# Second-half masked copies, ScalarE's copy of the queries' rope part, and GpSimd's subtraction of four levels' exponents, in the first mixer of a two-block model kernel

## The chip, the cores and the metric

The kernel is one program on one core of a Trainium2 chip. The metric is device time in microseconds (us) of one execution; lower is better. Five engines run their own instruction streams and meet at semaphores: TensorE (PE; its weight loads are listed apart as PEld), VectorE (DVE), ScalarE (ACT), GpSimd (POOL) and SyncE (SP, which issues DMAs). SBUF is the on-chip memory, PSUM the eight banks that TensorE writes to.

## The reference, cut to what matters

Two models of two layers follow each other, d_model 1024, batch 1, all float32. The sequence is 256 frames, with 16 meta tokens put in front in the first model: T = 272 columns. The change lies in one place, the first layer's mixer, which has two halves that read the same projection `z = rmsnorm(h) @ w_in`.

The first half is a gated linear recurrence (`hgrn2_mixer`), 4 heads of 128 keys and 128 values, in chunks of 64 tokens (the 16 meta tokens are a chunk of their own):

```python
b = jnp.cumsum(gi, axis=2)                        # sums of log decays in the chunk
diff = b[:, :, :, None, :] - b[:, :, None, :, :]
dec = jnp.exp(jnp.where(tri, diff, -jnp.inf))
att = jnp.einsum('bhtk,bhtsk,bhsk->bhts', qi, dec, ki)
o_intra = jnp.einsum('bhts,bhsv->bhtv', att, vi)
```

The second half is attention with low-rank queries and keys (`mla_mixer`), 4 heads; a head's query has 128 plain columns and 64 that are rotated (the rope part), and is normed over all 192 with a gain `qn_g` before the rotation.

Both halves' outputs go through `w_out`. What follows (the layer's MLP, the second layer and the second model) is not touched.

## The kernel before, in words

**Data.** Activations are kept feature by token: a tile holds 128 features by 272 tokens, and [128, 4, 272] holds all four heads. Weights come from HBM in units of up to 128x1024 through four buffers RAW (SP, `load_unit`). ScalarE copies a unit to a rounded half WH (`act_split`, L346) and VectorE subtracts it to get the rest, WL (`dve_split`, L353); each product is three matmuls (UH by WH, UL by WH, UH by WL; `products`, L368, and `products_rows`, L380). There are seven WH and WL buffers. Unit n of RAW is loaded once WL of unit n-4 is made; WH of unit n once the matmuls of unit n-7 are done. In the first mixer the units are: 10 and 11 the keys' and values' latent (`ckv`), 12 the keys' rope part (`kr`), 13 and 14 the queries (`qup`: plain and rope part), 15 the keys (`kvup` 0), 16 to 19 the recurrence's values (`hi`), 20 to 23 its gate (`hg`).

**The levels.** `att` inside a chunk can't be one product, since `dec` depends on both tokens. It is built in seven levels. Level 0 is the diagonal. Level number j (1 to 6) has the half size h = 1, 2, 4, 8, 16, 32: tokens are cut in blocks of 2h, and level j gives the pairs with the key's token s in a block's first half and the query's token t in its second half. With B the running sums and r the last token of the first half, the factor is exp(B[r]-B[s]) for a key and exp(B[t]-B[r]) for a query, both at most 1. For i = 0 to 5 (h = 1 to 32):

- `exponents(i)` on VectorE (L1145 to 1155) writes those two differences into E (even i) or HG (odd i); it waits for `scan` (B) and, from i = 2, for `op` i-2, which has read that buffer. For h up to 8 it is 2 instructions of 128x544, for h = 16 and 32 it is 8 of 128x128 (four heads, two halves).
- `exponents(i)` on ScalarE (L953 to 956) takes Exp of them in place.
- `operands(i)` on VectorE (L1157 to 1170) multiplies K and Q by them into KB and QB; it waits for ScalarE's Exp and until TensorE has read the last level's KB and QB (`mix atm`).
- `level(i)` on TensorE (L688, and L694 for the meta tokens) multiplies KB by QB: 16 weight loads and 16 matmuls of 128x128 into two PSUM banks.
- `attention(i+1)` on VectorE (L1177 to 1193) copies from these banks into ATT [128 keys' tokens, 8, 128 queries' tokens] where the mask `lev` of the level is set (`copy_predicated`, 2 instructions of 128x512, L1187), and likewise for the meta tokens (L1192). The masks of levels 1 to 6 have no bit in first halves of t.

**The queries' rope part.** TensorE's `up("qup", 1, ...)` leaves it in four PSUM banks. ScalarE's `query_rest` (L985) squares it into TMA (mark `hsq q 1`). VectorE's `query_rest` (L1253 to 1256) waits for that and copies it times the gain into QR (mark `gr q`). The banks are free for the keys' product `kvup` 0 at `gr q`; `kvup` 0 also needs the banks of the plain part, which ScalarE copies at L977.

**Order.** The order on each engine is written out by hand; there is no planner. VectorE, from the scan on: exponents 0, WL 11, exponents 1, operands 0, the latent's low parts (CL, L1197), attention 0, exponents 2, WL 12, CL, operands 1, attention 1, exponents 3, CL, `latent_pairs` (L1225), WL 13, `key_rest` (L1261), operands 2, attention 2, `latent_means` (L1207), exponents 4, WL 14, operands 3, attention 3, `latent_roots` (L1213 to 1218), exponents 5, WL 15, `query_rest`, operands 4, attention 4, the chunk's decay (L1396 to 1399), WL 16 and 17, `keys` (L1268), operands 5, attention 5, `head_pairs` q (L1231), attention 6, `head_pairs` k, WL 18, KD (L1413), and so on. TensorE: intra 0, `ckv` 1, level 0, `kr`, level 1, `latent_sums` (L709), `qup` 0, level 2, `qup` 1, level 3, `spread_columns` l (L746), `kvup` 0, level 4, values (0,0) (L380), level 5, values (0,1) with the queries' sums between (L724), `keys_turned` (L679, needs KD), further values, `rotate`. ScalarE around the change: Exp 0, WH 12, Exp 1, CH 2 (L970, L971), Exp 2, CH 3, WH 13 and 14, Exp 3, square of KR (L1048), WH 15, a root (L1051), the plain queries' copy and square (L977, L980), Exp 4, WH 16 and 17, `query_rest`, Exp 5, RKV (L1060), WH 18, the keys' square (L1064). GpSimd has only memsets: seven at the start of the mixer (L624 to 628) and two for the second model (L1698, L1699). SP only loads.

Of the kernel before, what the change touches and what calls it, by code (L numbers as in the profile page):

```python
# [8 lines left out]
T = 272  # L9
# [269 lines left out]
def program(nc, xin, pin, gains, cst, wpack, out):  # L279
# [13 lines left out]
    with ctx:  # L293
# [28 lines left out]
        def g(name, j=0, p=128):  # L322
            return G[0:p, GAT[name] + j:GAT[name] + j + 1]
# [297 lines left out]
        def gpsimd_mixer(p):  # L621
            for i, (z, val) in enumerate(((QB[:, :, :], 0.0), (KB[:, :, :], 0.0), (ATT[:, :, :], 0.0), (ATM[:, :, :], 0.0),
                                          (E[:, :, :], 1.0))):
                p.e.memset(z, val).then_inc(*p.mark("zero", i))  # L624
            p.wait_ge("zero", 4)
            p.e.memset(E[:, :, 0:1], 0.0).then_inc(*p.mark("zero", 5))
            p.wait_ge("zero", 5)
            p.e.memset(E[:, :, 16:T:64], 0.0).then_inc(*p.mark("zero", 6))


        def tensor_mixer(t):
# [144 lines left out]
            def rotate(key, src, nh):  # L776
                t.wait_ge("gr", key)
                b = banks.take(t, ("rot", key), ("rsin", key), nh)
                for hh in range(nh):
                    ins = t.e.matmul(PS[0:64, b + hh, 0:T], c("rot", p=64), src[:, hh, :], start=True, stop=True)  # L780
                ins.then_inc(*t.mark("mix", "rot", key))
# [88 lines left out]
            level(2)  # L870
            up("qup", 1, [(0, 0), (1, 1)], 64, ("gr", "q"))
            level(3)
# [78 lines left out]
        def scalar_mixer(a):  # L951
            def exponents(i):
                h, ee = LEVELS[i], EB[i % 2]  # L953
                rng = slice(0, T) if h <= 8 else slice(16, T)
                a.wait_ge("ex", i)
                a.e.activation(ee[:, :, rng], ee[:, :, rng], ACT.Exp).then_inc(*a.mark("exp", i))
# [25 lines left out]
            def query_rest():  # L982
                b1 = banks.at["qup", 1]
                a.wait_ge("mix", "qup", 1)
                a.e.activation(QRSQ[:, :, :], PS[0:64, b1:b1 + 4, 0:T], ACT.Square).then_inc(*a.mark("hsq", "q", 1))  # L985

# [153 lines left out]
        def vector_mixer(v):  # L1140
# [5 lines left out]
            def exponents(i):  # L1146
                h, ee = LEVELS[i], EB[i % 2]
                v.wait_ge("scan")
                if i > 1:
                    v.wait_ge("op", i - 2)  # L1150
                for (bl, br, ref), (el, er, _) in zip(halves(B, h), halves(ee, h)):
# [25 lines left out]
            def attention(level):  # L1177
# [5 lines left out]
                if level:  # L1183
                    v.wait_ge("att", level - 1)
                for x in range(2):
                    src = PS[:, b + x, :].rearrange("p (n t) -> p n t", t=128)
                    ins = v.e.copy_predicated(ATT[:, 4 * x:4 * x + 4, :], m, src)  # L1187
                if level <= 4:
# [63 lines left out]

            def query_rest():  # L1253
                b = banks.at["qup", 1]
                v.wait_ge("hsq", "q", 1)
                v.e.tensor_scalar(QR[:, :, :], PS[0:64, b:b + 4, 0:T], g("qr", 0, 64), None, ALU.mult).then_inc(
                    *v.mark("gr", "q"))

            def key_rest():
# [25 lines left out]
            def rotated(key, rr, nh):  # L1285
# [3 lines left out]
                v.wait_ge("c")  # L1289
                v.wait_ge("gr", key)  # L1290
                v.wait_ge("mix", "rot", key)
# [79 lines left out]
            attention(0)  # L1371
            exponents(2)
            dve_split(v, 13)
            latent(1, 0)
            operands(1)
            attention(1)
            exponents(3)
            latent(1, 1)
# [5 lines left out]
            latent_means()  # L1384
            exponents(4)
            dve_split(v, 15)
            operands(3)
            attention(3)
            latent_roots()
            exponents(5)  # L1390
            dve_split(v, 16)
            query_rest()
            operands(4)
# [1571 lines left out]
```

## Time and profile before

| | us |
|---|---|
| median of 3 runs | 1263.34 (1263.01 to 1263.54) |
| profiled execution: span of the instructions | 1261.9 |
| the profiled execution's own time beside its span | not listed; the median of the runs is 1.44 over the span |
| busy in the span: PE, PEld, DVE, ACT, POOL | 1231.6, 1206.4, 908.1, 737.1, 6.4 |
| granted TensorE clock, mean | 0.994 of full speed |
| DMA | 205.51 MB, mean 163 GB/s |

Busy times are sums over instructions that overlap a little in their pipelines, so the step from one instruction's start to the next one's start is the better price where an engine runs without a pause. "Idle before" is the pause in front of an instruction with what released it. PEld, the weight loads, shows TensorE's pauses more plainly than the matmuls, whose ends are modelled.

### The profile page before, as it was taken

What the parts mean: (1) busy time and instruction counts of PE and PEld (TensorE: products, weight loads), DVE (VectorE), ACT (ScalarE), POOL (GpSimd) and SP (SyncE); (2) the same over time, 40 slices, a digit from 0 to 9 for tenths busy, and PEclk for the clock granted to TensorE, in tenths of its full rate; (3) what the DMA queues carried; (4) which work ended last, traced back from release to release, by engine and by line L of the source; (5) the groups of instructions that cost most, each with busy time, mean ns of one, the idle gap of its engine ahead of it and who ended that gap; (6) DMA issues with size and microseconds to landing.
All of it is one profiled execution on the core that took longest, in us unless ns stands there. A gap on an engine that the chain in (4) does not pass through costs nothing.

```text
span 1261.9 us, 24318 instructions
## 1 busy us (share of the span) xinstructions
PE 1231.6 (98%) x10110; PEld 1206.4 (96%) x10110; DVE 908.1 (72%) x1571; ACT 737.1 (58%) x1257; POOL 6.4 (1%) x16
## 2 busy tenths in 40 slices
PE   8999999999999999999999999999999999999997
PEld 8889799999999999999999999999888899999997
DVE  6896566665446776444876899966788768999656
ACT  6753456664445765334555666655766866665655
POOL 1000000000000000000000000000000000000000
PEclk9999999999999999999999999999899999999999
DMA  7223244555552655553663666574364236665640
GB/s 275 72 101 105 64 164 148 192 181 180 174 168 98 216 186 185 184 184 126 218 195 119 193 194 199 159 238 134 120 225 159 89 117 192 193 189 188 215 141 34
DMA packets 59753, 205.51 MB, mean 163 GB/s; under 512 B 6739, under 2 KB 9340, under 8 KB 59516
## 3 DMA queue, kind: packets, MB, share of 16 engines
q1 hardware_dynamic: 57536, 201.21, 49.0%
q10 hardware_dynamic: 2108, 2.75, 0.7%
q8 instruction: 80, 1.31, 0.4%
q14 instruction: 29, 0.24, 0.1%
HBM read 202.87 MB, written 1.06 MB: 162 GB/s over the span
## 4 chain that ended last, share of the span: by engine, by line
PE 85%; DVE 8%; ACT 4%; issue 1%; DMA 1%; DVEq 0%; ACTq 0%
PE PS L368 69%; PE PS L413 6%; DVE WL L353 2%; PE PS L380 2%; DMA RAW<-wpack 1%; ACT WH L346 1%; PE PS L462 1%; PE PS L2450 1%; ACT EE L2608 1%; PE PS L520 1%; PE PS L2517 0%; PE PS L688 0%; DVE X L1905 0%; ACT L532 0%; PE PS L402 0%
## 5 line engine op out<-in xcount | busy, mean ns | idle before, releaser
L353 DVE TENSOR_TENSOR WL<-RAW,WH 128x1024 fp32r<-128x1024 f32 (+2 forms) x387 | 460.6, 1195 | 211.3 <-ACT WH L346 210.8
L346 ACT ACTIVATE WH<-RAW 128x1024 fp32r<-128x1024 f32 (+2 forms) x387 | 392.3, 1033 | 218.6 <-PE PS L368 184.8
L368 PE MATMUL PS<-UH,WH 128*128 128x256 f32 (+1 forms) x1464 | 415.7, 284 | 7.6 <-DVE WL L353 3.8
L368 PE MATMUL PS<-UL,WH 128*128 128x256 f32 (+1 forms) x1464 | 414.9, 283 | 0.0
L368 PE MATMUL PS<-UH,WL 128*128 128x256 f32 (+1 forms) x1464 | 414.7, 283 | 0.0
L368 PEld LDWEIGHTS PS<-UH,WH 128*128 128x128 f32 x1464 | 276.6, 189 | 8.6 <-issue 3.4
L368 PEld LDWEIGHTS PS<-UH,WL 128*128 128x128 f32 x1464 | 276.9, 189 | 0.0
L368 PEld LDWEIGHTS PS<-UL,WH 128*128 128x128 f32 x1464 | 275.2, 188 | 0.0
L368 PE MATMUL PS<-HL,WH 128*128 128x272 f32 (+1 forms) x512 | 145.8, 285 | 0.0
L368 PE MATMUL PS<-HH,WH 128*128 128x272 f32 (+1 forms) x512 | 145.6, 284 | 0.0
L368 PE MATMUL PS<-HH,WL 128*128 128x272 f32 (+1 forms) x512 | 145.4, 284 | 0.0
L368 PE MATMUL PS<-FH,WH 128*128 128x256 f32 x352 | 98.5, 280 | 0.0
L368 PE MATMUL PS<-FL,WH 128*128 128x256 f32 x352 | 98.5, 280 | 0.0
L368 PE MATMUL PS<-FH,WL 128*128 128x256 f32 x352 | 98.5, 280 | 0.0
L368 PEld LDWEIGHTS PS<-HH,WL 128*128 128x128 f32 x512 | 96.6, 189 | 0.0
L368 PEld LDWEIGHTS PS<-HL,WH 128*128 128x128 f32 x512 | 96.3, 188 | 0.0
L368 PEld LDWEIGHTS PS<-HH,WH 128*128 128x128 f32 x512 | 96.1, 188 | 0.0
L413 PE MATMUL PS<-UH,WH 128*128 128x256 f32 (+1 forms) x240 | 68.7, 286 | 1.5 <-DVE UL L540 1.2
L413 PE MATMUL PS<-UL,WH 128*128 128x256 f32 (+1 forms) x240 | 67.6, 282 | 0.0
L413 PE MATMUL PS<-UH,WL 128*128 128x256 f32 (+1 forms) x240 | 67.6, 282 | 0.0
L368 PEld LDWEIGHTS PS<-FH,WH 128*128 128x128 f32 x352 | 66.2, 188 | 0.0
L368 PEld LDWEIGHTS PS<-FL,WH 128*128 128x128 f32 x352 | 66.2, 188 | 0.0
(409 smaller groups left out, 2066.1 us busy)
## 6 DMA issues: line engine op xcount, KB each, us to landing
RAW<-wpack SPq DMA_DIRECT2D x361, 512.0 KB, 4.2
RAW<-wpack SPq DMA_DIRECT2D x18, 384.0 KB, 3.5
RAW<-wpack SPq DMA_DIRECT2D x6, 256.0 KB, 2.7
C<-cst SPq DMA_DIRECT2D x1, 1072.0 KB, 5.9
HB<-bias_rows ACTq DMA_DIRECT2D x1, 1024.0 KB, 5.3
out<-X SPq DMA_DIRECT2D x4, 256.0 KB, 2.3
X<-xin ACTq DMA_DIRECT2D x2, 272.0 KB, 6.0
X<-xin SPq DMA_DIRECT2D x2, 272.0 KB, 5.9
```

Source lines behind the costliest of these rows:

```text
L346: a.e.activation(WH[n % NH][:, 0:w], RAW[n % NR][:, 0:w], ACT.Copy).then_inc(*a.mark("wh", n))
L353: v.e.tensor_tensor(WL[n % NH][:, 0:w], RAW[n % NR][:, 0:w], WH[n % NH][:, 0:w].bitcast(f32), ALU.subtract).then_inc(*v.mark("wl", n))
L368: ins = t.e.matmul(o, part(n, hw, kw, a, b), x(kx), start=first and not i and not p, stop=last and i == len(kcs) - 1 and p == 2)
L380: ins = t.e.matmul(o, x(kx), part(n, hw, kw, 0, w), start=not i and not p, stop=i == len(kcs) - 1 and p == 2)
L413: ins = t.e.matmul(PS[:, b, 0:w], part(n, hw, k, 0, 128), x_(k), start=k == 0 and p == 0, stop=k == 7 and p == 2)
L462: return t.e.matmul(o, src[:, m, a:z], ONE[:, 0:1], start=start, stop=stop)
L520: ins = t.e.matmul(PS[:, b, a:z], rooted(st, x).to_broadcast([128, 128]), ID[:, 0:z - a], start=True, stop=True)
L2450: ins = t.e.matmul(PS[:, b, 0:256], x[:, k, 128 * i:128 * i + 128], part(n, hw, kw, 0, 256), start=k == 0 and p == 0, stop=k == 7 and p == 2)
L2608: ins = a.e.activation(e, e, ACT.Exp, bias=s[:, 2 * i + m:2 * i + m + 1], scale=-1.0, accum_out=s[:, 4 + 2 * i + m:5 + 2 * i + m])
```

## The change

Four edits, all in the first mixer.

1. `exponents(i)` for i = 2 to 5 (h = 4, 8, 16, 32) leaves VectorE and is issued by GpSimd with the same tiles and shapes, in this order, each behind `op` i-2. Its mark is `exg`, and ScalarE's Exp of these four waits for it. 20 instructions in all: 2, 2, 8 and 8.
2. `attention` for levels 1 to 6 copies second halves of t only: one instruction over both banks, of 128 x 8 x (64/h) x h = 128x512 elements, in place of two of 128x512. Level 0 stays as it was, the meta tokens' copies too.
3. QR, the queries' rope part times its gain, is copied by ScalarE in its `query_rest`, ahead of the square, and VectorE's `query_rest` is gone. The banks of `qup` 1 are free at ScalarE's square.
4. The waits on QR go by ScalarE's new mark (`qn` 1).

```diff
@@ gpsimd_mixer
             p.e.memset(E[:, :, 16:T:64], 0.0).then_inc(*p.mark("zero", 6))
+            p.wait_ge("scan")
+            for i in range(2, 6):
+                h, ee = LEVELS[i], EB[i % 2]
+                p.wait_ge("op", i - 2)
+                for (bl, br, ref), (el, er, _) in zip(halves(B, h), halves(ee, h)):
+                    rb = ref.to_broadcast(list(bl.shape))
+                    p.e.tensor_tensor(el, rb, bl, ALU.subtract)
+                    ins = p.e.tensor_tensor(er, br, rb, ALU.subtract)
+                ins.then_inc(*p.mark("exg", i))
@@ tensor_mixer (and the same in VectorE's rotated)
-                t.wait_ge("gr", key)
+                t.wait_ge(*(("qn", 1) if key == "q" else ("gr", key)))
@@
-            up("qup", 1, [(0, 0), (1, 1)], 64, ("gr", "q"))
+            up("qup", 1, [(0, 0), (1, 1)], 64, ("hsq", "q", 1))
@@ scalar_mixer
-                a.wait_ge("ex", i)
+                a.wait_ge("ex" if i < 2 else "exg", i)
@@
                 a.wait_ge("mix", "qup", 1)
+                a.e.activation(QR[:, :, :], PS[0:64, b1:b1 + 4, 0:T], ACT.Copy, scale=g("qr", 0, 64)).then_inc(*a.mark("qn", 1))
                 a.e.activation(QRSQ[:, :, :], PS[0:64, b1:b1 + 4, 0:T], ACT.Square).then_inc(*a.mark("hsq", "q", 1))
@@ vector_mixer, attention
-                for x in range(2):
-                    src = PS[:, b + x, :].rearrange("p (n t) -> p n t", t=128)
-                    ins = v.e.copy_predicated(ATT[:, 4 * x:4 * x + 4, :], m, src)
+                h = 1 << level >> 1
+                if level == 0:
+                    for x in range(2):
+                        src = PS[:, b + x, :].rearrange("p (n t) -> p n t", t=128)
+                        ins = v.e.copy_predicated(ATT[:, 4 * x:4 * x + 4, :], m, src)
+                else:
+
+                    def second(z):
+                        return z.rearrange("p (n k s) -> p n k s", n=8, s=2 * h)[:, :, :, h:2 * h]
+                    mh = c("lev", 128 * level, 128 * level + 128).bitcast(u32).rearrange("p (k s) -> p k s", s=2 * h)[:, :, h:2 * h]
+                    k, w = mh.shape[1], mh.shape[2]
+                    ins = v.e.copy_predicated(second(ATT[:, :, :].rearrange("p n t -> p (n t)")),
+                                              mh.unsqueeze(1).to_broadcast([128, 8, k, w]),
+                                              second(PS[:, b:b + 2, :].rearrange("p x t -> p (x t)")))
@@ the order on VectorE
-            exponents(2)
...
-            exponents(3)
...
-            exponents(4)
...
-            exponents(5)
             dve_split(v, 16)
-            query_rest()
             operands(4)
```

## Rows read from the trace of the kernel before

**Rows 1.** The page: span, busy time by engine, chain that ended last.
```profile
span 1261.9 us, 24318 instructions
PE 1231.6 (98%) x10110; PEld 1206.4 (96%) x10110; DVE 908.1 (72%) x1571; ACT 737.1 (58%) x1257; POOL 6.4 (1%) x16
PE 85%; DVE 8%; ACT 4%; issue 1%; DMA 1%; DVEq 0%; ACTq 0%
```
**Rows 2.** Windows: length, busy PE, PEld, DVE, ACT, POOL, clock, DMA share, GB/s.
```profile
46.00:85.42 39.42, 33.73 (x298) 31.70 (x298) 38.61 (x89) 24.68 (x35) 0.00 (x0) 1.00 0.26 90
85.42:146.30 60.88, 60.88 (x471) 54.96 (x472) 39.85 (x61) 26.05 (x42) 0.00 (x0) 1.00 0.31 98
```
**Rows 3.** Timeline of TensorE's weight loads: start, length, [idle before <-releaser].
```profile
56.59 0.13 PEld L368 LDWEIGHTS PS<-UH,WH 128*64 128x64 f32 x1 [1.65 <-DVE CL L1197]
73.73 0.74 PEld L746 LDWEIGHTS PS<-ID,CO 128*128 128x128 f32 x6
75.88 0.19 PEld L368 LDWEIGHTS PS<-CH,WH 128*128 128x128 f32 x1 [1.41 <-DVE QR L1256]
78.93 1.86 PEld L688 LDWEIGHTS PS<-QB,KB 128*128 128x128 f32 x16
81.47 0.09 PEld L380 LDWEIGHTS PS<-WH,UH 128*16 128x16 f32 x1 [0.68 <-DVE WL L353]
85.42 1.86 PEld L688 LDWEIGHTS PS<-QB,KB 128*128 128x128 f32 x16 [1.34 <-DVE QB L1169]
```
**Rows 4.** VectorE's groups by form, 47 to 94 us: busy, mean ns.
```profile
L1187 DVE COPY_PREDICATED ATT<-C,PS 128x512 f32<-128x512 uint32 x14 | 9.4, 721 | 0.0
```
**Rows 5.** VectorE's timeline around steps of the sum (start, length).
```profile
47.06 0.73 DVE L1153 TENSOR_TENSOR E<-B 128x544 f32<-128x544 f32 x1
54.18 0.71 DVE L1153 TENSOR_TENSOR E<-B 128x544 f32<-128x544 f32 x1
55.45 0.67 DVE L353 TENSOR_TENSOR WL<-RAW,WH 128x512 fp32r<-128x512 f32 x1
68.61 0.72 DVE L1168 TENSOR_TENSOR KB<-K,HG 128x544 f32<-128x544 f32 x1 [0.71 <-PE PS L694]
71.74 0.28 DVE L1153 TENSOR_TENSOR HG<-B 128x128 f32<-128x128 f32 x1
73.36 1.22 DVE L353 TENSOR_TENSOR WL<-RAW,WH 128x1024 fp32r<-128x1024 f32 x1
74.49 1.34 DVE L1256 TENSOR_SCALAR QR<-PS,G 64x1088 f32<-64x1088 f32 x1
75.75 0.27 DVE L1168 TENSOR_TENSOR KB<-K,E 128x128 f32<-128x128 f32 x1
77.37 1.34 DVE L1187 COPY_PREDICATED ATT<-C,PS 128x512 f32<-128x512 uint32 x2
80.21 2.34 DVE L353 TENSOR_TENSOR WL<-RAW,WH 128x1024 fp32r<-128x1024 f32 x2
82.48 1.27 DVE L1268 TENSOR_TENSOR KN<-PS,ACC 128x1088 f32<-128x1088 f32 x1
91.57 1.27 DVE L1413 TENSOR_TENSOR K<-K,E 128x1088 f32<-128x1088 f32 x1
```
**Rows 6.** ScalarE's timeline: the plain queries' copy, and the rope part's square.
```profile
66.46 1.08 ACT L977 ACTIVATE QN<-PS 128x1088 f32<-128x1088 f32 x1 [0.43 <-PE PS L368]
73.00 1.05 ACT L985 ACTIVATE TMA<-PS 64x1088 f32<-64x1088 f32 x1
```
**Rows 7.** GpSimd's timeline: memsets at the start and late.
```profile
0.98 1.00 POOL L624 MEMSET QB<- 128x1088 f32 x1
1.92 1.00 POOL L624 MEMSET KB<- 128x1088 f32 x1
284.71 0.95 POOL L1698 MEMSET V0H<- 128x1024 f32 x1 [279.53 <-PE PS L368]
```
**Rows 8.** VectorE's timeline beside the last of these memsets.
```profile
285.05 1.49 DVE L1650 TENSOR_TENSOR HL<-TB,HH 128x272 fp32r<-128x272 f32 x4
```

More of the change, by code:

```diff
@@ L1148, in exponents @@
                 v.wait_ge("scan")
-                if i > 1:
-                    v.wait_ge("op", i - 2)
                 for (bl, br, ref), (el, er, _) in zip(halves(B, h), halves(ee, h)):
@@ L1251, in key_roots @@
                 v.e.reciprocal(KSC[:, :, :], KSC[:, :, :]).then_inc(*v.mark("hrec", "k"))
[L1253 to L1257, printed above, removed]
             def key_rest():
@@ L1289, in rotated @@
                 v.wait_ge("c")
-                v.wait_ge("gr", key)
+                v.wait_ge(*(("qn", 1) if key == "q" else ("gr", key)))
                 v.wait_ge("mix", "rot", key)
```

## The prediction

> **What bounds the kernel now.** I read the page first: TensorE is busy 98% of the 1261.9 us span, and the chain that ended last runs 85% on TensorE, 8% on VectorE [rows 1]. So VectorE's work is free except where TensorE pauses for it, and the question is whether the first mixer is such a place. The windows say so, and where it stops: from 46.00 to 85.42 us VectorE is busy 38.61 of 39.42 us and TensorE 33.73; from 85.42 to 146.30 TensorE is busy all 60.88 us, VectorE 39.85 and ScalarE 26.05, so neither of these is short of time [rows 2]. Third, the weight loads, which show what ends each pause: in the first stretch there are four pauses that VectorE ends, 1.65 us before `kr` (a latent's low part, CL), 1.41 us before `kvup` 0 (QR), 0.68 us before the values (WL 16) and 1.34 us before level 5 (QB) [rows 3]. Their sum, 5.08 us, is the most that relief of VectorE can bring here. After 85.42 us all depends on TensorE, and the weight stream is tied to WL and to used buffers, not to the clock on the wall; so what level 5's start gains, the end gains. The sum below is of level 5's start (85.42 us).
>
> **What is taken from VectorE.** Levels 4 and 8: two instructions of 128x544 each, 1.27 us for the pair (54.18 to 55.45, start to start). Levels 16 and 32: eight of 128x128 each, 1.62 us (71.74 to 73.36) [rows 5]. Together 2 x 1.27 + 2 x 1.62 = 5.78 us. QR: 1.26 us (74.49 to 75.75) [rows 5]. Masked copies: two of 128x512 take 1.24 us by start spacing (two of 0.72 us, overlapping) [rows 4, 5], so one takes 0.62, and one goes in each of levels 1 to 6, four of them ahead of level 5. The strides in the new copy are new for this instruction. Bounds: 0.62 us if an element costs what it does now, 1.24 if strided reads of PSUM halve the rate. I take 0.62: the subtractions in runs of one and of four take 0.73 and 0.71 us for 544 elements, so short runs cost VectorE next to nothing in SBUF, and the masked copy in whole rows, 0.72 for 512, is the nearest row in kind [rows 4, 5]. Ahead of level 5 this makes 5.78 + 1.26 + 4 x 0.62 = 9.5 us of VectorE's time, against 5.08 us of pauses: TensorE and the remaining order will set the gain, not the sum.
>
> **Step 1, up to `kr`.** `kr` waits for CL of latent 1,0, behind exponents 2 and WL 12 on VectorE. Without exponents 2 it comes 1.27 us earlier, 56.59 becomes 55.32, and 0.38 of the 1.65 us is left [rows 3, 5]. From here TensorE runs through level 1, the latent sums, `qup` 0, level 2, `qup` 1, level 3 without a pause (no other pause stands between the first two of rows 3 that have one), so all of it moves by 1.27 us. VectorE is now ahead: at operands 3 it already waited 0.71 us for TensorE [rows 5], and from now on operands 2, 3 and 4 wait for TensorE's last level.
>
> **Step 2, `kvup` 0.** Its banks come free at ScalarE's square of the rope part, no longer at VectorE's copy of it. ScalarE reaches that place 6.54 us after the plain copy's start (66.46 to 73.00) with a root's tables and two WH between [rows 6]; the plain copy moves with TensorE by 1.27 us. The new copy there costs about what the square of the same shape does, 1.05 us, or 0.96 by start spacing. So the square ends at 73.00 + 1.05 - 1.27 + 1.0 = 73.8, and `kvup` 0 starts 2.1 us earlier than its 75.88. TensorE could have been there at 74.47 - 1.27 = 73.2: ScalarE's copy isn't hidden wholly, 0.6 us of the pause stay. They cost nothing if step 3 is later anyway, which it is.
>
> **Step 3, from operands 4 to level 5.** Operands 4 need level 3's products. TensorE has them at 73.73 [rows 3], 72.46 now. From operands 4 to level 5's start VectorE works without a pause, 75.75 to 85.42 = 9.67 us [rows 3, 5]: operands 4, masked copy, decay, WL 16 and 17, KN, operands 5. One 0.62 goes: 9.05 us, so level 5 starts at 72.5 + 9.05 = 81.55. Beside it TensorE: level 4 at 78.93 - 2.08 = 76.85, the values behind it at 78.8 (WL 16 is ready at 77.5, that pause goes), 2.6 us for them, over at 81.4. The two meet within 0.2 us, VectorE last. KN's input is ready at 76.9, VectorE comes to it at 78.6. Level 5: 85.42 - 81.55 = 3.87 us earlier. KD, which `keys_turned` needs, began 6.15 us behind level 5's start [rows 3, 5]; two masked copies of 0.62 stand in that stretch, so it has room.
>
> **Step 4, what GpSimd costs.** The trace has no subtraction on GpSimd, only memsets: 1088 elements in 0.94 us by start spacing, 0.47 us for 544, 0.11 for 128 [rows 7]. That is the low end; three streams (two in, one out) at that price each make 1.41 and 0.33, with some 0.04 between instructions 0.37. I take 1.2 and 0.33 us as an estimate, nearer to the upper end, since a subtraction has all three streams: 2.4 us for a pair, 2.6 us for eight. Without a clash with VectorE this is hidden everywhere, at both ends. Exponents 2 start at operands 0's end (52.0) and are there at 54.4, where they came at 55.4. Exponents 3 start at 56.5 and are used by operands 3 at 67. Exponents 4 start at 61.8, end at 64.4, and ScalarE comes to their Exp only at 68.5. Exponents 5 start at 68.6, end at 71.2, ScalarE comes at 73.8. The cover is gone only at over 2.2 us for 128x544, or 0.9 for 128x128.
>
> **Step 5, the clash.** When GpSimd last worked beside VectorE, four VectorE subtractions with both inputs in SBUF began 0.34 us into a memset (284.71) and took 1.49 us, 0.37 each, as without it [rows 7, 8]. A memset reads nothing. If a subtraction on GpSimd keeps VectorE's two-input work out while it runs, the work beside it counts. Exponents 2: VectorE has CL, CL and the whole masked copies of level 0, which read PSUM, up to 54.18; GpSimd is through at 54.4; 0.25 us is lost ahead of `kr`. Exponents 3 and 4: `latent_pairs` and WL 14 slip by 1.5 to 2 us, into VectorE's new waits for TensorE. Exponents 5: operands 3 end at 68.9, GpSimd holds to 71.5, then roots and WL 15 (1.6 us) end at 73.1, where operands 4 could start at 72.75: 0.35 us. So 0.6 us lost: 3.3 us gained instead of 3.9. I take the middle, 3.6 us.
>
> The Trainium skill, "SBUF — State Buffer", section "Who interferes with whom", says just that: VectorE and GpSimd share a port pair, whichever takes it holds it for its whole instruction, and a VectorE instruction with two SBUF inputs contends with GpSimd's reads but not with its writes. Rows 7 and 8 agree with the second half; nothing in the trace of before shows the first. Its "GPSIMD Engine Reference", section "Performance versus the Vector engine", has 4497 ns for GpSimd's addition of two tensors of 2048 elements a partition, about 1.2 us for 544; the sum would be the same by it.
>
> The profiled execution's span is 1261.9 us, the median of the runs 1263.34, 1.44 more that lies around it; the same is taken for after. Forecast: 1263.34 - 3.6 = 1259.7 us.
>
> **Rivals.**
> (a) Half of it is lost to the clash. Same mechanism, GpSimd at 1.4 us and 0.45 to 0.5: exponents 2 hold WL 12 to 54.85 (0.7 us lost ahead of `kr`), exponents 5 end at 73, roots and WL 15 at 74.9 where 73.1 was wanted (1.7 us). Gain 1.2 to 2 us: 1261.7. For: two readers, all of VectorE's work there is two-input. Against: that price is above my upper end.
> (b) Slower. The place is the eight small instructions: if one has a fixed cost that a memset doesn't show, at 0.9 us each exponents 4 hold VectorE for 7.2 us from 62.6 to 69.8, WL 14 ends at 70.4 where `qup` 1 wanted it at 67.4 (3 us), and exponents 5 from 71.7 to 78.9, WL 15 at 80.5 where `kvup` 0 started at 75.88. Level 5 is then 4.6 us later than before: 1267.9. It decides from about 0.63 us for a 128x128, with the clash; without it only beyond 1.2 us. For: VectorE itself takes 0.20 us (1.62 / 8) for 128 elements where the share of its 544 would be 0.15, and GpSimd's fixed part is unknown for this operation. Against: the two memsets of 1088 follow each other at 0.94 us, which leaves little that is fixed [rows 7].
> (c) The masked copies aren't shorter (runs of 1, 2, 4 elements). Then VectorE's last stretch is 9.67 again: 0.6 us less, 1260.3. Against: VectorE's subtraction in runs of one takes 0.73 us for 544, that in runs of four 0.71 [rows 5].
>
> **How the numbers follow.** Forecast 0.52 (own range 1259.2 to 1260.6); (a) 0.24; (b) 0.14; (c) 0.10. No-change is within 0.2%, 2.5 us, about what a measurement of this kernel can tell. Faster by more: the forecast, (c), a little of (a) cut off below: 0.61. Within: (a) and the mild part of (b): 0.26. Slower: 0.13. Range: from 4.3 us gained (all of steps 1 to 3, and a little of ScalarE's gap) to none, 1259.0 to 1263.3; outside lie (b) and a few per cent below.
>
> **What would show it.** `kr` starts near 55.4, `kvup` 0 near 73.8, level 5 near 81.7 (with the first 46 us as they were), and no pause on TensorE behind it. VectorE waits for TensorE at operands 2, 3 and 4. GpSimd's 128x544 at 1.1 to 1.4 us, its 128x128 at 0.3 to 0.4. One masked copy a level at 0.7 us. The clash: WL 12, `latent_pairs`, WL 14 and WL 15 start only when GpSimd's set ends, or last longer than their 0.67 and 1.22 us. Wrong it would be if level 5 comes after 83 us, or if TensorE meets new pauses behind it.

## The result, and the profile after

| | before | changed |
|---|---|---|
| the first measurement, 4 runs each | 1263.17 us (1262.01 to 1263.54) | 1258.34 us (1256.62 to 1259.85) |
| the same kernels once more, 26 and 12 runs | 1262.01 us (1260.60 to 1264.45) | 1257.92 us (1256.72 to 1263.38) |
| span of the profiled execution | 1261.9 us | 1257.4 us |

The ratio of the first measurement is 0.9963, 95% interval 0.9950 to 0.9976; that of the second 0.9969, 0.9959 to 0.9979: 3.9 us faster (1262.01 x 0.0031), between 2.7 and 5.2. The forecast was 1259.7 us with a range from 1259.0: the direction and nearly all the steps came as forecast, the measured time lies 0.7 us below the range. Times of further runs below are medians, with their ratio to the kernel before.

Each run lists its time and the span of its instructions. The time is 2.08 to 2.21 us over the span in every one of 42 runs of the kernel before, and 1.76 to 1.88 in every one of 21 of the changed kernel (five of them with more idle matmuls at the start, e10 below). So about 0.33 us of the gain lies outside the span. The spans themselves differ by 3.4 us between the means (1260.0 and 1256.6) and by 3.75 between the medians (1259.85 and 1256.1) of the 26 and 12 runs.

TensorE's pauses of 0.2 us and more before level 5 show where the time went. Timeline of TensorE's weight loads of the changed kernel, with the starts of `kr`, `kvup` 0 and `level(5)` and in front of them the first load of the diagonal's product (`intra(0, K, Q)`, called level 0 below) (start, length, [idle before <-releaser]):

```profile
45.19 1.86 PEld L697 LDWEIGHTS PS<-Q,K 128*128 128x128 f32 x16 [0.28 <-issue]
54.84 0.13 PEld L368 LDWEIGHTS PS<-UH,WH 128*64 128x64 f32 x1 [0.71 <-DVE CL L1216]
73.42 0.19 PEld L368 LDWEIGHTS PS<-CH,WH 128*128 128x128 f32 x1 [0.76 <-ACT TMA L995]
81.20 1.86 PEld L697 LDWEIGHTS PS<-QB,KB 128*128 128x128 f32 x16 [0.25 <-DVE QB L1177]
```

And the same first load in the kernel before:

```profile
46.02 1.86 PEld L688 LDWEIGHTS PS<-Q,K 128*128 128x128 f32 x16 [0.28 <-issue]
```

The four pauses of before, 5.08 us [rows 3], have become 0.71 + 0.76 + 0.25 = 1.72 us; that of WL 16 is gone. All of them depend on what comes after level 0, so the fair clock for them starts there: level 5 began 85.42 - 46.02 = 39.40 us after level 0, and now begins 81.20 - 45.19 = 36.01 us after it. That is 3.39 us. The other 0.83 us by which level 5 is earlier was there before level 0, in code that the change does not touch. Windows of the two traces (length, busy PE, PEld, DVE, ACT, POOL, granted clock, DMA share, GB/s), before and then changed:

```profile
8.00:12.00 4.00, 4.00 (x21) 4.00 (x22) 3.07 (x8) 3.80 (x8) 0.00 (x0) 0.60 1.05 420
```

```profile
8.00:12.00 4.00, 3.63 (x28) 3.42 (x28) 2.99 (x8) 3.71 (x8) 0.00 (x0) 1.00 1.04 418
```

In the execution before, TensorE had been idle for 2.44 us ahead of its first tile at 7.84 us and then was granted 0.60 of full speed in this window, mostly its lower level of 1.2 GHz: 22 weight loads in 4 us. In the changed kernel's execution, idle for 1.62 us there, it had all of its 2.4 GHz: 28 loads in 4 us. That is a difference between two executions, not between two kernels.

VectorE and GpSimd in the stretch. VectorE's timeline, changed kernel:

```profile
53.37 1.00 DVE L353 TENSOR_TENSOR WL<-RAW,WH 128x512 fp32r<-128x512 f32 x1
55.97 1.34 DVE L1204 COPY_PREDICATED ATT<-C,PS 128x512 f32<-128x512 uint32 x1
57.62 1.36 DVE L1244 TENSOR_TENSOR CQ<-CQ 128x544 f32<-128x544 f32 x1
61.66 1.32 DVE L1204 COPY_PREDICATED ATT<-C,PS 128x512 f32<-128x512 uint32 x1
62.97 0.67 DVE L353 TENSOR_TENSOR WL<-RAW,WH 128x512 fp32r<-128x512 f32 x1
66.87 0.73 DVE L1176 TENSOR_TENSOR KB<-K,HG 128x544 f32<-128x544 f32 x1 [3.23 <-PE PS L703]
68.15 0.71 DVE L1204 COPY_PREDICATED ATT<-C,PS 128x512 f32<-128x512 uint32 x1
69.08 0.37 DVE L1234 TENSOR_TENSOR CO<-CO,RS 128x6 f32<-128x6 f32 x1
69.74 1.21 DVE L353 TENSOR_TENSOR WL<-RAW,WH 128x1024 fp32r<-128x1024 f32 x1
72.10 0.35 DVE L1176 TENSOR_TENSOR KB<-K,E 128x128 f32<-128x128 f32 x1 [1.14 <-PE PS L703]
86.53 1.27 DVE L1421 TENSOR_TENSOR K<-K,E 128x1088 f32<-128x1088 f32 x1
```

GpSimd's timeline, changed kernel:

```profile
51.43 1.09 POOL L635 TENSOR_TENSOR E<-B 128x544 f32<-128x544 f32 x1 [46.25 <-DVE QB L1177]
52.48 1.34 POOL L636 TENSOR_TENSOR E<-B 128x544 f32<-128x544 f32 x1
57.19 1.22 POOL L636 TENSOR_TENSOR HG<-B 128x544 f32<-128x544 f32 x1
62.90 1.02 POOL L636 TENSOR_TENSOR E<-B 128x128 f32<-128x128 f32 x1
69.39 0.41 POOL L636 TENSOR_TENSOR HG<-B 128x128 f32<-128x128 f32 x1
69.76 1.45 POOL L635 TENSOR_TENSOR HG<-B 128x128 f32<-128x128 f32 x1
```

The second instruction of a 128x544 pair starts 1.05 us after the first, and one of 128x128 about 0.36 us after another. Two things are to be seen. First the clash, in both directions. WL 12 (0.67 us before, [rows 5]) lasts 1.00 beside GpSimd's second instruction, which ends at 53.82. `latent_pairs` (0.70 us before) lasts 1.36 and ends 0.57 us after GpSimd's (58.98 and 58.41). Of GpSimd's instructions the one at 69.76 lasts 1.45 us, to 0.26 us behind the end of WL 15, which began 0.02 us before it. The recorded starts do not tell who waits: at 62.90 GpSimd's 128x128 began 0.07 us before WL 14, and it lasted 1.02 us, again to 0.28 us behind the other's end, while WL 14 kept its 0.67. Instructions of VectorE that read PSUM beside GpSimd's first pair, from 51.43 to 53.82, kept their lengths: two CL took 0.90 us together and the two masked copies of level 0 1.33, as in the kernel before. Second the masked copies: 0.70 to 0.74 us from level 3 on, but 1.34 and 1.32 at levels 1 and 2, for one instruction of half the elements. VectorE waits 3.23 and 1.14 us for TensorE at operands 3 and 4; at operands 2 it does not, they start at 60.39 right behind KR.

### The profile page after: what moved, and what is told of

Read it like the earlier page. It is cut to its first block, busy times and chain, and to the rows that moved or that the text cites. A ratio compares the mean times of both kernels' runs of the same rounds, so it can differ in the third digit from the quotient of the medians.

```text
span 1257.4 us, 24316 instructions
## 1 busy us (share of the span) xinstructions
PE 1230.4 (98%) x10110; PEld 1205.3 (96%) x10110; DVE 899.8 (72%) x1544; ACT 738.2 (59%) x1258; POOL 18.6 (1%) x36
## 3 DMA queue, kind: packets, MB, share of 16 engines
q8 instruction: 80, 1.31, 0.4%
HBM read 202.87 MB, written 1.06 MB: 162 GB/s over the span
## 4 chain that ended last, share of the span: by engine, by line
PE 84%; DVE 7%; ACT 6%; DMA 2%; issue 1%; ACTq 0%; DVEq 0%; SPq 0%
PE PS L368 68%; PE PS L413 7%; PE PS L380 2%; DVE WL L353 2%; ACT WH L346 2%; DMA RAW<-wpack 1%; PE PS L462 1%; PE PS L2458 1%; ACT EE L2616 1%; PE PS L520 1%; ACT L532 1%; DMA X<-xin 1%; DVE X L1913 1%; PE PS L2525 0%; PE PS L697 0%
```

## The experiments

Each was compared with the kernel before on the same chip. "Level 5" is the start of `level(5)`'s first load counted from level 0's, as above: 39.40 us in the kernel before. In the timeline of weight loads it was 36.01, 36.00 and 36.01 in three traces of the changed kernel (one of them with more idle matmuls at the start) and 39.42 in a second one of the kernel before. e5 to e8 were run once each, beside one run of the kernel before (1265.04 us). Their times, 1259.43, 1257.36, 1259.50 and 1263.97 us in this order, decide little, since single runs of one kernel differ by more than 3 us; these four are read from their traces.

**e1_again.** The changed kernel with no edit.

> The changed kernel once more, with more runs. Theory A (the prediction's steps were right, and the rest of the 4.8 us came from TensorE's clock at the start): in the first two traces the clock stood at its lower level from 7.8 to 11.2 us in the kernel before and not in the changed one, and this made 0.85 us of the 4.5 us between the spans; the start of level 5, counted from the start of level 0's loads, moved by 3.4 us. So the gain here: 3.3 to 3.9 us if this lower stretch comes as often in the one as in the other, and in every trace level 5 stands 3.4 us (within 0.1) earlier counted from level 0. Theory B (the changed kernel saves more than the prediction's steps, somewhere behind level 5): a gain of 4.5 us or more also where both have the same start, growing along the span.

1257.92 against 1262.01 us, ratio 0.9969 (0.9959 to 0.9979). Level 5 at 80.75 - 44.75 = 36.00 us. Theory A's number for the steps holds to 0.01 us; its time, 3.3 to 3.9, is met by 3.9, and B's 4.5 lies inside the interval, so the times alone don't exclude it. The spans speak against it, with means 3.4 us apart for 3.4 us at level 5, though their blur leaves room for about 1 us either way. From level 5 to the end the traces leave 1176.5 and 1177.6 us in two executions of the kernel before, 1176.2, 1177.3 and 1174.8 in three of the changed one, and 1173.9 to 1177.6 in the other versions: the tail differs by 2.5 us among executions of the changed kernel alone, so no gain of some tenths can be read there. In the first 22 us of it the two kernels are alike: the load at 107.74 us before and at 103.47 in the changed kernel comes 22.32 and 22.27 us after level 5. In the unchanged tail, TensorE's clock is one thing that differs between executions. Windows of the kernel before and then of e1_again:

```profile
890.00:915.00 25.00, 23.67 (x171) 21.91 (x170) 19.76 (x39) 18.46 (x36) 0.00 (x0) 0.86 0.42 136
```

```profile
890.00:915.00 25.00, 23.46 (x157) 21.70 (x156) 18.51 (x41) 17.17 (x36) 0.00 (x0) 0.80 0.29 96
```

0.80 of full speed and 157 matmuls in e1_again, 0.86 and 171 in the kernel before. It does not account for all of it: the 1177.6 us of the kernel before come from a trace with 0.86 there.

**e2_gpsimd_only, e3_no_gpsimd, e4_whole_copies.** The change in parts.

```diff
# e2_gpsimd_only: the kernel before, with the subtractions of levels 4 to 32 on GpSimd, and nothing else
# e3_no_gpsimd: the changed kernel, with these back on VectorE, in their old places
-                a.wait_ge("ex" if i < 2 else "exg", i)
+                a.wait_ge("ex", i)
# e4_whole_copies: the changed kernel, the masked copies of all levels as before
+                for x in range(2):
+                    src = PS[:, b + x, :].rearrange("p (n t) -> p n t", t=128)
+                    ins = v.e.copy_predicated(ATT[:, 4 * x:4 * x + 4, :], m, src)
```

> Only the subtractions of levels 4 to 32 go to GpSimd; masked copies whole, QR on VectorE. Theory A (each edit takes VectorE's time, and TensorE's order caps the sum): kr 1.0 to 1.3 us earlier, level 5 some 1.9 us earlier counted from level 0, time 1.9 us under before. Theory B (GpSimd's subtractions cost VectorE as much as they take from it): within 0.7 us of before.

> Second-half copies and QR on ScalarE, the subtractions stay on VectorE. Theory A: kr not earlier, kvup 0 about 1.0 us, level 5 some 2.4 us earlier, time 2.4 us under before. The masked copies of levels 1 and 2 took 1.34 and 1.32 us in the changed kernel, those of levels 3 to 6 0.70 to 0.74. If that is the runs of one and two elements, they take 1.3 us here too, with GpSimd silent; if it is GpSimd's reading beside them, all six take 0.7 here.

> The changed kernel with whole masked copies at all levels. Theory A: only the copy of level 4, in the unbroken stretch from operands 4 to level 5, matters: 0.6 us slower than the changed kernel, 2.9 us under before. Theory B (copies of all six levels count, 0.6 us each where they were halved): 2.4 us slower than the changed kernel.

| | us, median (runs) | ratio to before (95%) | level 5 | expected |
|---|---|---|---|---|
| e2_gpsimd_only | 1259.62 (11) | 0.9982 (0.9973 to 0.9990) | 38.09: 1.31 earlier | 1.9 |
| e3_no_gpsimd | 1259.22 (8) | 0.9975 (0.9965 to 0.9985) | 36.88: 2.52 earlier | 2.4 |
| e4_whole_copies | 1258.32 (5) | 0.9966 (0.9954 to 0.9978) | 36.66: 2.74 earlier | 2.8 |

The masked copies are worth 36.66 - 36.01 = 0.65 us, the one copy in the stretch behind operands 4, as theory A had it; the time differs by too little to be told from none. All three times agree with what theory A gave, within their intervals. GpSimd's part is worth 36.88 - 36.01 = 0.87 us on top of the rest, and 1.31 alone. That is less than expected, and the VectorE timeline of e2 says why:

```profile
72.00 1.34 DVE L1263 TENSOR_SCALAR QR<-PS,G 64x1088 f32<-64x1088 f32 x1 [1.04 <-ACT TMA L994]
```

QR on VectorE waits for ScalarE's square. In the kernel before the square ended at 74.05 us and VectorE came to QR only at 74.49 [rows 5, 6]; relieved, VectorE comes first and stands 1.04 us, and the whole stretch from operands 4 on stands behind it. Masked copies in e3, with GpSimd silent (VectorE's timeline, levels 1, 2, 3):

```profile
56.38 1.30 DVE L1197 COPY_PREDICATED ATT<-C,PS 128x512 f32<-128x512 uint32 x1
62.68 1.30 DVE L1197 COPY_PREDICATED ATT<-C,PS 128x512 f32<-128x512 uint32 x1
68.53 0.71 DVE L1197 COPY_PREDICATED ATT<-C,PS 128x512 f32<-128x512 uint32 x1
```

So it is not GpSimd that makes levels 1 and 2 long.

**e5_qr_back.** QR's copy back on VectorE, behind ScalarE's square, with the waits on it as before; all else as changed.

```diff
-                a.e.activation(QR[:, :, :], PS[0:64, b1:b1 + 4, 0:T], ACT.Copy, scale=g("qr", 0, 64)).then_inc(*a.mark("qn", 1))
...
+            query_rest()
             operands(4)
```

> The changed kernel with QR's copy back on VectorE (still behind ScalarE's square). Counted from level 0's loads, level 5 started 39.40 us later before and 36.01 and 36.00 in two traces of the changed kernel. Theory A: the copy stands in front of operands 4 on VectorE and kvup 0 waits for it, 1.0 us of the gain goes: 37.0. Theory B (ScalarE's copy gives nothing, since the pause before kvup 0 stays at 0.76 us, now for ScalarE): 36.0 to 36.2.

Level 5 at 82.72 - 45.28 = 37.44 us: theory A, but 1.43 us dearer than the changed kernel in place of 1.0. The reason is that of e2, here 1.40 us of waiting (VectorE's timeline):

```profile
72.43 1.34 DVE L1274 TENSOR_SCALAR QR<-PS,G 64x1088 f32<-64x1088 f32 x1 [1.40 <-ACT TMA L994]
```

**e6_memsets.** GpSimd writes a constant instead of the differences; this leaves out the subtractions of levels 4 to 32.

```diff
-                    p.e.tensor_tensor(el, rb, bl, ALU.subtract)
-                    ins = p.e.tensor_tensor(er, br, rb, ALU.subtract)
+                    p.e.memset(el, -1.0)
+                    ins = p.e.memset(er, -1.0)
```

> The subtractions of levels 4 to 32 are left out: GpSimd writes a constant to the same places with memsets of the same shapes. In the changed kernel latent_pairs took 1.36 us instead of 0.70 and WL 12 1.00 instead of 0.67 beside GpSimd's subtractions. If it is GpSimd's reading of SBUF that holds VectorE's two-input work, both are back at 0.70 and 0.67 here, kr comes 0.3 us earlier and level 5 at 35.6 to 35.7 us from level 0. If any work on GpSimd does it, they stay long. The masked copies of levels 1 and 2 stay at 1.3 us in both.

```profile
54.05 0.67 DVE L353 TENSOR_TENSOR WL<-RAW,WH 128x512 fp32r<-128x512 f32 x1
56.33 1.30 DVE L1204 COPY_PREDICATED ATT<-C,PS 128x512 f32<-128x512 uint32 x1
57.97 0.70 DVE L1244 TENSOR_TENSOR CQ<-CQ 128x544 f32<-128x544 f32 x1
```

(VectorE's timeline; the rows answer to the first three of the changed kernel above.) WL 12 is back at 0.67 and `latent_pairs` at 0.70; the pause before `kr` is 0.39 us instead of 0.71, level 5 at 35.62, as expected. But a memset is also shorter than a subtraction. GpSimd's timeline, the second of each pair:

```profile
52.57 0.55 POOL L636 MEMSET E<- 128x544 f32 x1
56.95 0.55 POOL L636 MEMSET HG<- 128x544 f32 x1
```

The first pair is over at 53.12 us, before WL 12 begins, and the second at 57.50, before `latent_pairs`. So these two say only that the clash costs 0.39 us of level 5 in all, not what in GpSimd's work makes it. The roots and WL 15 say more, because memsets did run beside them (e6, VectorE's timeline, then GpSimd's):

```profile
69.45 0.17 DVE L1234 TENSOR_TENSOR CO<-CO,RS 128x6 f32<-128x6 f32 x1
69.65 0.16 DVE L1237 TENSOR_TENSOR CO<-CO 128x3 f32<-128x3 f32 x1
69.73 1.22 DVE L353 TENSOR_TENSOR WL<-RAW,WH 128x1024 fp32r<-128x1024 f32 x1
```

```profile
69.49 0.21 POOL L635 MEMSET HG<- 128x128 f32 x1
69.63 0.21 POOL L636 MEMSET HG<- 128x128 f32 x1
```

The two roots take 0.17 and 0.16 us, as in the kernel before, and WL 15 and the memset beside its start keep their lengths; beside subtractions, in the changed kernel, the same two roots took 0.37 and 0.33 us and GpSimd's instruction beside WL 15 1.45. With [rows 7, 8] this makes it GpSimd's reading of SBUF, and not any work of it, that clashes.

**e7_patterns.** Other addresses in the masked copies of one instruction each; so ATT is not the reference's.

```diff
+                    h = 1 if level != 5 else 2
...
+                    fo = dense if level in (2, 4) else second
+                    fs = dense if level in (1, 3) else second
...
+                    if level in (3, 4):
+                        mh = m2[:, 0:64].rearrange("p (k s) -> p k s", s=h)
```

> The changed kernel with other addresses in the masked copies of 512 elements, so what they pick is not the reference's. Runs of one with stride two, unless said: level 1 out and mask strided, PSUM source dense; level 2 mask and source strided, out dense; level 3 only out strided; level 4 only the source; level 5 all three in runs of two; level 6 all three in runs of one. Theory P (reading short runs from PSUM costs double): levels 2, 4, 5, 6 take 1.3 us, 1 and 3 0.7. Theory O (the write to SBUF, which also has to keep what isn't masked): 1, 3, 5, 6 take 1.3, 2 and 4 0.7. Theory M (the mask): 1, 2, 5, 6 take 1.3, 3 and 4 0.7.

VectorE's timeline, levels 1 to 6:

```profile
55.59 1.32 DVE L1215 COPY_PREDICATED ATT<-C,PS 128x512 f32<-128x512 uint32 x1
61.27 0.72 DVE L1215 COPY_PREDICATED ATT<-C,PS 128x512 f32<-128x512 uint32 x1
67.76 1.35 DVE L1215 COPY_PREDICATED ATT<-C,PS 128x512 f32<-128x512 uint32 x1
73.39 0.73 DVE L1215 COPY_PREDICATED ATT<-C,PS 128x512 f32<-128x512 uint32 x1
80.70 1.30 DVE L1215 COPY_PREDICATED ATT<-C,PS 128x512 f32<-128x512 uint32 x1
83.05 1.29 DVE L1215 COPY_PREDICATED ATT<-C,PS 128x512 f32<-128x512 uint32 x1
```

1.32, 0.72, 1.35, 0.73, 1.30, 1.29: theory O in all six. In these rows, reading PSUM or the mask with a stride costs nothing (0.72 and 0.73 us), and writing SBUF in runs of one or two floats nearly doubles the masked copy (1.29 to 1.35). The subtraction of level 1, which writes with the same stride, takes 0.73 us for 544 elements [rows 5], so it is this instruction and not the stride as such.

**e8_twice.** GpSimd does the 128x128 subtractions twice, the extra ones into tiles not yet in use (shortened).

```diff
+                    if h >= 16:
+                        for y, (z0, z1) in enumerate(((rb, bl), (br, rb))):
...
+                            p.e.tensor_tensor(spare[:, at:at + 128]..., z0, z1, ALU.subtract)
```

> The changed kernel in which GpSimd does each 128x128 subtraction of levels 16 and 32 twice, the extra ones into tiles not yet in use: 16 in place of 8 a level, so GpSimd is busy some 5.9 us for each. Theory A (a held engine waits for one instruction of the other at most, and VectorE gets in between two of GpSimd's): WL 14, the roots and WL 15 slip by under 0.5 us, level 5 stays at 36.0 to 36.4 us from level 0. Theory B (rival b of the prediction: GpSimd's whole set holds VectorE): WL 15 only when the set ends, level 5 some 4.5 us later, 40.5 to 41.1.

Both theories failed on level 5. It comes at 39.49 us, 3.5 late, but WL 15 is on time (70.44 - 45.69 = 24.75 us from level 0; 24.55 in the changed kernel). GpSimd's timeline, and VectorE's beside it:

```profile
76.23 0.40 POOL L641 TENSOR_TENSOR HG<-B 128x128 f32<-128x128 f32 x1
76.59 4.15 POOL L642 TENSOR_TENSOR HG<-B 128x128 f32<-128x128 f32 x1
```

```profile
73.47 0.49 DVE L1182 TENSOR_TENSOR KB<-K,E 128x128 f32<-128x128 f32 x1
73.88 0.48 DVE L1183 TENSOR_TENSOR QB<-Q,E 128x128 f32<-128x128 f32 x1
76.66 0.21 DVE L1410 TENSOR_TENSOR E<-B 128x64 f32<-128x64 f32 x1
76.79 1.41 DVE L1413 TENSOR_TENSOR E<-B 128x256 f32<-128x256 f32 x4
78.13 2.34 DVE L353 TENSOR_TENSOR WL<-RAW,WH 128x1024 fp32r<-128x1024 f32 x2
82.22 1.29 DVE L1287 TENSOR_TENSOR KN<-PS,ACC 128x1088 f32<-128x1088 f32 x1 [1.75 <-ACT ACC L1076]
```

The last of GpSimd's 128x128 was held from 76.59 to 80.74 us, through seven two-input instructions of VectorE without a gap, and with it Exp 5, RKV behind it on ScalarE, KN and level 5. In operands 4 the two took turns instead: VectorE's start every 0.41 us, twice the 0.20 of before, while GpSimd's start every 0.41 too. Why turns there and none here stays open. The delay did not end with the late start (TensorE's weight loads in e8):

```profile
85.18 3.24 PEld L703 LDWEIGHTS PS<-QB,KB 128*128 128x128 f32 x16 [2.80 <-DVE QB L1183]
```

After this pause of 2.80 us the granted clock was 0.56 of full speed from 85.18 to 88.50 us, nearly its lower level, and level 5's 16 loads took 3.24 us instead of 1.86: 1.38 us more, on top of the 3.5. It is what the kernel before's execution did at 7.84 us, after an idle of 2.44 us.

**e9_before_warm, e10_after_warm.** 36 instead of 24 idle matmuls (matmuls whose results nobody uses) in front of the first tile.

```diff
-            keep_going(t, 24)
+            keep_going(t, 36)
```

> The kernel before with 36 instead of 24 idle matmuls on TensorE ahead of the first tile. In its first trace TensorE stood idle for 2.4 us at 5.4 to 7.8 us and its clock was at the lower level from 7.8 to 11.2 us; that cost 0.85 us against a trace without the stretch. Theory A (this lottery at the start is what blurs the comparison): no lower stretch between 7 and 12 us, time 0 to 0.9 us under before, by how often the stretch comes without it. Theory B: the stretch comes all the same, no difference.

> The changed kernel with the same 36 idle matmuls. Theory A: level 5 at 36.0 us from level 0's loads, as in every trace of it, and 3.4 to 3.9 us under the kernel before with 36. Theory B (the changed kernel's gain is 4.5 us or more): so much more than that under it.

Before: 1261.73 against 1261.97 us, ratio 0.9999 (0.9990 to 1.0008). Changed: 1257.90, ratio to the unwarmed kernel before 0.9969 (0.9957 to 0.9981), 3.8 us under the warmed one by medians, and level 5 at 36.01 us: e10's theory A. The two theories of e9 are not told apart by its time. But its spread did not shrink (1260.63 to 1264.48 in 11 runs), and the execution that was traced, the slowest of them at 1264.48 us, had a granted clock of 1.00 from 8 to 12 us. So the lower stretch at the start explains the 0.83 us between the two first traces, but not the blur of the times.

**e11_reordered, e12_reordered_warm.** The three pauses left over, by order alone; the second with 36 idle matmuls.

```diff
             exponents(1)
+            dve_split(v, 13)
             operands(0)
             latent(0, 0)
             latent(0, 1)
+            latent(1, 0)
             attention(0)
-            dve_split(v, 13)
-            latent(1, 0)
@@ ScalarE
-            act_split(a, 18)
             query_rest()
+            act_split(a, 18)
@@ the decay moves from ahead of dve_split(v, 18) to behind head_pairs("q", ...)
```

> The changed kernel with the three pauses that are left taken out by order alone: VectorE makes WL 12 ahead of operands 0 and the third CL ahead of the masked copy of level 0, ScalarE does QR and its square ahead of WH 16 and 17, VectorE computes the decay behind the queries' head_pairs. Theory A (these three waits, 0.71, 0.76 and 0.25 us, are all that is left before level 5): no pause over 0.1 us before kr, kvup 0 and level 5; level 5 at 34.3 us from level 0 instead of 36.0, KD with 0.1 us to spare; 1.5 to 1.7 us faster than the changed kernel. Theory B (WL 12 or KD is late in its new place and makes a pause of its own): less than 1 us faster.

> Both: the reordered kernel with 36 idle matmuls. Theory A: 5.0 to 6.5 us under before, 0 to 0.9 us under the reordered one.

1257.28 us (6 runs), ratio 0.9962 (0.9950 to 0.9974), and 1256.22 us (5 runs), 0.9956 (0.9944 to 0.9969): the fastest versions measured, 4.7 and 5.75 us under before by medians. Level 5 is at 80.51 - 45.69 = 34.82 us, 1.19 us better than the changed kernel in place of 1.7. The pauses before `kr`, `kvup` 0 and level 5 are gone, and one came where there was none, ahead of the code's `level(0)` (not the diagonal's product that the times are counted from), which needs operands 0 (TensorE's weight loads in e11):

```profile
52.90 1.86 PEld L697 LDWEIGHTS PS<-QB,KB 128*128 128x128 f32 x16 [0.48 <-DVE QB L1177]
```

WL 12 ahead of operands 0 costs there what it saves `kr`, but for 0.2 us. So theory B of e11 is the nearer one: in its new place WL 12 makes a pause of its own. The gain in time over the changed kernel is 0.6 us by medians, B's "less than 1 us", but not told from none: the intervals overlap. e12 lies 5.75 us under before, as its theory A had it, and 1.06 us under e11, where it had 0 to 0.9, a difference within the same blur.

## Why the prediction was wrong in its time and right in most of its steps

**The sum's terms**, counted from level 0 (the prediction's times minus 46.02, the traces' minus 45.19):

| step | predicted, no clash / clash | measured |
|---|---|---|
| 1, `kr` starts | 9.30 / 9.55 | 9.65 |
| 2, `kvup` 0 starts | 27.8 | 28.23 |
| 3, operands 4 start | 26.5 / 27.1 | 26.91 |
| 3, from there to level 5 | 9.05 | 9.10 |
| level 5 starts | 35.5 / 36.15 | 36.01 |

Step 1: 0.38 us of the pause was to stay, and 0.25 more with the clash; 0.71 stayed. e6 gives the clash its size, 0.34 us here (`kr` at 55.19 - 45.88 = 9.31) and 0.39 for level 5, where 0.6 was worked out. The second half of that, WL 15 held by exponents 5, did not come: the roots in front of it took 0.37 us more in all, but WL 15 kept its 1.21 us while GpSimd waited, and operands 4 then had TensorE to wait for. So one half was too small (0.25 for 0.34) and the other (0.35) was not there; that their sum came near is in part luck. Step 2: ScalarE's copy and square are the pause at `kvup` 0, 0.76 us for the 0.6 predicted, and it cost level 5 nothing, as said: TensorE still had 0.25 us to wait there, for VectorE. Step 4: 1.05 and 0.36 us for the 1.2 and 0.33 estimated, inside both bounds; but with the instructions that VectorE held, the sets of eight took 3.6 and 4.0 us where 2.6 was worked out, which stayed hidden. Step 3 is right to 0.05 us. KD had room: it ended at 87.80, and the loads that wait for it start at 88.53. So level 5 gained 3.39 us; the value taken was 3.6.

**Masked copies.** 0.62 us at all six levels was wrong at levels 1 and 2: by start spacing 1.12 and 1.11 us (1.34 and 1.32 by length), near the upper bound of 1.24. At levels 3 and 4 it is 0.60. The argument for 0.62 was read from subtractions with short runs, and e7 shows that these say nothing about a masked write. It cost nothing: operands 2 did not have to wait for TensorE in the changed kernel, but TensorE was busy without a pause from `kr` to `kvup` 0. Rival (c), the copies are no shorter, is thus half true, and its price was for level 4, where they are shorter.

**Rivals (a) and (b).** Neither came, though the mechanism of both, the ports held, is there. They had VectorE held by GpSimd's whole set; the runs show instructions held one at a time, in turns, or GpSimd held by VectorE. That GpSimd's long set would be slow, (b), is true in e8, but by another way: GpSimd's result is late for ScalarE.

**The step that failed** is the one from the sum to the time: "The profiled execution's span is 1261.9 us, the median of the runs 1263.34, 1.44 more that lies around it; the same is taken for after. Forecast: 1263.34 - 3.6 = 1259.7 us", with a range that gave the lower side only "4.3 us gained". Two things in it were wrong. The median of three from which it subtracts was high: 26 and 16 later runs of the kernel before have 1262.01 and 1261.97. Whether chance or the chip made the three high is not on record. And the 1.44 us compared the span of one execution with the time of others. Within one run 2.08 to 2.21 us lie outside the span in the kernel before, and 1.76 to 1.88 in the changed one, so the same is not to be taken for after: 0.33 us of gain stand in no step of the sum. Why is open. e2, which only moves work to GpSimd, and e3, which moves none there, both have 1.82 on average, and the kernel before keeps 2.13 with more idle matmuls. The 3.39 us of steps and this 0.33 under 1262.01 make 1258.3, where the changed kernel measured 1258.34 and 1257.92. The range was made of the steps' bounds alone, although 26 runs of the kernel before on one chip differ by up to 3.9 us (1260.60 to 1264.45), and medians of a few of them by some tenths to over 1 us. Against the 3.9 us (2.7 to 5.2) of time, 3.72 are accounted for; the rest is not told from noise.

The Trainium skill, "SBUF — State Buffer", section "Who interferes with whom", has the ports held for a whole instruction by whichever took them. The changed kernel's trace agrees in that one of the two instructions is held until the other is over (1.36 us in place of 0.70, 1.45 in place of 0.40); which of them took the ports first, its recorded starts do not show. e8's 4.15 us goes beyond it, since seven instructions passed while one waited.

## What to carry to other kernels

Count a relieved stretch from a point that the change cannot move, and separately from what came earlier; then a tenth of a microsecond can be read from one trace each (36.00 and 36.01 us in three traces), where the times of single runs differ by several. Taking work from the engine that ends the waits pays until the next engine ends them: here about 8.6 us of VectorE's were taken (5.78 of subtractions, 1.26 of QR, 1.55 of masked copies ahead of level 5, all by start spacing; 9.5 were forecast) and 3.4 came out, and the QR copy was worth 1.43 us, more than its length, because it stood behind ScalarE. Put what goes to GpSimd where VectorE reads PSUM (0.90 and 1.33 us there, as without it), and where its result is needed only well later: in e8 it had to let 3.8 us of two-input work pass. Before a forecast is subtracted from a median, ask how far medians of so few runs lie apart, and compare spans with spans and times with times.

## What the runs showed of the hardware that was not expected

- A masked copy whose output in SBUF has runs of one or two floats takes 1.29 to 1.35 us for 128x512; with runs of four and more, or dense, 0.70 to 0.74. Strides in its PSUM source or mask change nothing (0.72, 0.73). A subtraction with the same output stride is not slowed (0.73 for 544 elements).
- GpSimd's subtraction of 128x128 was held 4.15 us by seven VectorE instructions with two SBUF inputs in a row, and elsewhere in the same trace the two engines took turns, each starting every 0.41 us. VectorE's two-input instructions beside GpSimd's memsets kept their lengths.
- After pauses of TensorE of 2.44 us (kernel before) and 2.80 us (e8) the granted clock was 0.60 and 0.56 over the next 4.0 and 3.3 us; after 1.62 us (changed kernel) it was 1.00.
- In code that no version changes, from level 5 to the end, the traces took 1173.9 to 1177.6 us, and TensorE's granted clock from 890 to 915 us was 0.80 in three of them (e1, e3, e7), 1.00 in one (e6) and 0.86 in the others.
- The time that lies outside the span of the instructions was 2.08 to 2.21 us in every run of the kernel before and 1.76 to 1.88 in every run of every edited version but e9.
